# Fourier branch folded by symmetry, 20 modulation blocks moved, one bank wait shortened

## The reference, cut to what matters

```python
hl = modulate(rms_norm(xl, g_mix_norm[l]), sh1, sc1)
pl = hl @ wl                              # q, k, v and a Fourier part fl of 4 groups x 128
mix_l = concatenate([diff_attention(ql, k_all, v_all, lam, g_subln[l], lambda_init),
                     fourier_mix(fl, w_fourier[l])], axis=-1)
xl = xl + gt1 * (mix_l @ w_out[l])
...
def fourier_mix(f, w_fourier):
    fg = f.reshape(b, n, 4, 128).astype(float32)
    fr = fft2(fg, axes=(1, 3), norm='ortho').real       # over 512 tokens and 128 channels
    return einsum('bngc,gcd->bngd', fr, w_fourier).reshape(b, n, 512)
...
mod = silu(c) @ ada_w[i] + ada_b[i]       # second block: 6 x 1024 values, 48 blocks of 128
```

## Time and profile before

| | before |
|---|---|
| median of 3 runs | 2212.67 us |
| the profiled execution's own time | 2213.58 us |
| its span | 2211.9 us |
| mean granted PE clock | 0.992 |
| ACT busy | 702.6 us (32%) |
| DMA moved | 434.71 MB |
| first scores of the attention steps | 118 us from the start |

### The profile page before, as it was taken

How to read it: one execution, slowest core, us unless ns; L and a number is a source line. 1 busy time by engine, 2 the same in 40 slices (tenths; PEclk the granted TensorE clock), 3 DMA queues, 4 the chain that set the end, 5 groups by cost and what they waited for, 6 DMA issues and landing times.

```text
span 2211.9 us, 24806 instructions
## 1 busy us (share of the span) xinstructions
PE 2134.6 (97%) x9914; PEld 1428.7 (65%) x9914; DVE 1215.4 (55%) x1726; ACT 702.6 (32%) x1059; POOL 148.8 (7%) x157
## 2 busy tenths in 40 slices
PE   7999998997999989999999999999999999999997
PEld 3454444333333335678888888878777788888886
DVE  1776863344433336895474555566986646343434
ACT  4123422110000005323242231346884424232331
POOL 0011100002310004000000000000110000000000
PEclk9999999999999999999999999999999999999999
DMA  9756465999999993211345454423342222222221
GB/s 389 288 185 215 142 241 208 401 427 427 420 426 426 428 427 127 79 68 62 133 160 186 156 177 163 143 77 116 126 156 81 96 95 77 95 95 95 95 96 57
DMA packets 112808, 434.71 MB, mean 197 GB/s; under 512 B 7982, under 2 KB 13106, under 8 KB 98760
## 3 DMA queue, kind: packets, MB, share of 16 engines
q1 hardware_dynamic: 92872, 361.46, 42.6%
q0 software_dynamic: 19840, 71.93, 9.0%
HBM read 430.57 MB, written 6.36 MB: 198 GB/s over the span
## 4 chain that ended last, share of the span: by engine, by line
PE 60%; PEld 15%; DVE 7%; DMA 7%; issue 6%; ACT 2%; DVEq 2%; POOLq 0%; SPq 0%; PEldq 0%; POOL 0%; ACTq 0%
PE PS L1132 7%; PE PS L740 6%; PE PS L743 6%; PE PS L744 6%; PE PS L840 6%; PEld PS L740 5%; PEld PS L744 5%; PEld PS L743 4%; DMA work<-in_w_dn 4%; PE PS L1155 4%; PE PS L1399 3%; PE PS L1403 3%; PE PS L1402 3%; PE PS L1169 2%; PE PS L969 2%
## 5 line engine op out<-in xcount | busy, mean ns | idle before, releaser
L744 PE MATMUL PS<-work_f32r,work_f32r 128*128 128x512 f32 x1168 | 454.4, 389 | 0.0
L2155 DVE TENSOR_TENSOR ring_f32r<-ring,work_f32r 128x2048 fp32r<-128x2048 f32 x100 | 227.8, 2287 | 140.5 <-ACT work_f32r L1553 140.1
L740 PE MATMUL PS<-work_f32r,work_f32r 128*128 128x512 f32 x768 | 299.5, 390 | 2.1 <-DVE work_f32r L2902 1.1
L743 PE MATMUL PS<-work_f32r,ring_f32r 128*128 128x512 f32 x768 | 298.8, 389 | 0.0
L1553 ACT ACTIVATE work_f32r<-ring 128x2048 fp32r<-128x2048 f32 x100 | 190.2, 1910 | 304.0 <-DMA ring<-in_mlp_w 247.0
L744 PEld LDWEIGHTS PS<-work_f32r,work_f32r 128*128 128x128 f32 x1168 | 219.3, 188 | 45.6
L1132 PE MATMUL PS<-work 128*64 128x512 f32 x752 | 170.6, 597 | 2.2 <-ACT work L1761 2.2
L740 PEld LDWEIGHTS PS<-work_f32r,work_f32r 128*128 128x128 f32 x768 | 144.2, 188 | 33.3 <-DVE work_f32r L2902 1.5
L743 PEld LDWEIGHTS PS<-work_f32r,ring_f32r 128*128 128x128 f32 x768 | 144.2, 188 | 29.8 <-issue 0.2
L740 PE MATMUL PS<-h_f32r,work_f32r 128*128 128x512 f32 x400 | 155.9, 390 | 1.4 <-DVE work_f32r L2175 1.4
L743 PE MATMUL PS<-h_f32r,ring_f32r 128*128 128x512 f32 x400 | 155.6, 389 | 0.0
(11 more groups left out here) (423 smaller groups left out, 3357.8 us busy)
## 6 DMA issues: line engine op xcount, KB each, us to landing
work<-in_w_gu SPq DMA_DIRECT2D x47, 2048.0 KB, 21.9
ring<-in_mlp_w SPq DMA_DIRECT2D x64, 1024.0 KB, 5.2
work<-in_w_dn SPq DMA_DIRECT2D x24, 2048.0 KB, 24.6
ring<-in_w_gu SPq DMA_DIRECT2D x16, 2048.0 KB, 24.2
work<-in_ada_w_2T POOLq DMA_DIRECT2D x48, 512.0 KB, 3.6
work<-in_ada_w_2T POOLq DMA_DIRECT2D x16, 1536.0 KB, 6.8
ring<-in_m_w_in SPq DMA_DIRECT2D x20, 1024.0 KB, 5.2
work<-in_w_adaT POOLq DMA_DIRECT2D x8, 2048.0 KB, 10.4
```

The lines of the kernel that those rows point to most:

```text
L740: mm = nc.tensor.matmul(PS[:, bank + k, :], f32r(w_of), f32r(hi(c)), start=first and c == 0, stop=False)
L743: nc.tensor.matmul(PS[:, bank + k, :], f32r(wlo), f32r(hi(c)), start=False, stop=False)
L744: mm = nc.tensor.matmul(PS[:, bank + k, :], f32r(w_of), f32r(lo(c)), start=False, stop=last and c == 3)
L2155: tt(f32r(ring[:, s, at, :]), ring[:, s, at, :], f32r(tiles[s][:, at, :]), ALU.subtract).then_inc(w_split, 1)
```

## The change

The diff has three parts.

1. **The Fourier branch is folded.** Tokens t and 512 − t have the same cosine and opposite sines. DVE forms sum and difference of the two halves (`fold_tokens`, three instructions of up to 255 columns for each group); PE then has 5 matmuls of 128 columns for the channels and 5 of 255 or 257 columns for the tokens, all in banks 0 and 1; ACT copies 512 and 257 columns; DVE makes the 512 output frequencies from 257 cosine and 255 sine ones (`unfold_frequencies`, two instructions, one operand in PSUM, one side read backwards). Group g now has its channels and tokens in step 9 + g and `mix_out` at the start of step 10 + g. The value projections are spread as 2, 1, 1, 1, 1 over steps 0 to 4 and the projections of the Fourier part stand in steps 5 to 8. Part of out_part(0, 1) moves from step 15 to step 13.
2. **20 of the 48 modulation blocks leave the steps.** The steps keep 28 (`BLOCKS_AT`). The other 20 are 10 pairs, loaded by POOL as 1024 KB each into two new buffers, the first two when head 2's product is done, pair j when pair j − 2 has been used. DVE works pairs 2c and 2c + 1 ahead of the addition of output chunk c, for c = 0 to 4. The addition of their bias and the gain that needs them move to the gated stage of the second block.
3. **The wait of bank 7.** `head_values` waits for `ovar_ready` (the end of `head_var`, which reads the bank) in place of `head_done`.

```diff
-ADA_BLOCKS = NMOD * KC
-ADA_DONE = ADA_LATE + ADA_BLOCKS
+ADA_IN_STEPS = 28
+ADA_PAIRS = (NMOD * KC - ADA_IN_STEPS) // 2
+ADA_DONE = ADA_LATE + ADA_IN_STEPS + ADA_PAIRS
...
-        dft_c, dft_s, dft_ch = wk(13312, TC, T), wk(15360, TC, T), wk(17408, 256)
-        fab, fre = wk(17664, 2, 4, 256), wk(19712, T)
+        dft_c, dft_s, dft_ch = wk(13312, 3, 257), wk(14088, 2, 255), wk(17408, 256)
+        f_odd, f_half, fab, fre = wk(14600, GROUPS, 256), wk(16648, GROUPS, P), wk(15624, 2, 4, P), wk(19712, T)
...
+        ada_pair = [wk(17664, 2, D), wk(30720, 2, D)]
...
+        FIRST_MIX = 9
...
+        def mirrored(v):
+
+            n = v.ap[-1][1]
+            return bass.AP(v.tensor, v.offset + n - 1, [v.ap[0], (-1, n)])
...
-            sp.wait_ge(ada_used, 2 + ADA_DONE)
+            sp.wait_ge(ada_used, 2 + ADA_LATE + ADA_IN_STEPS)
...
-            for q in range(ADA_BLOCKS):
+            for q in range(ADA_IN_STEPS):
                 pool.wait_ge(ada_used, 2 + ADA_LATE + max(q - 1, 0))
                 pool.dma_start(ada_block[q % 2], A["ada_w_2T"][0, q * P:(q + 1) * P, :]).then_inc(ada_loaded[q % 2], 16)
-
-
-            pool.wait_ge(zero_row_stored, 16)
-            pool.wait_ge(rows_stored, 16)
+            pool.wait_ge(pv_mm, HEADS - 1)
+            for j in range(ADA_PAIRS):
+                pool.wait_ge(ada_used, 2 + ADA_LATE + ADA_IN_STEPS + max(j - 1, 0))
+                pool.dma_start(ada_pair[j % 2], A["ada_w_2T"][0, (ADA_IN_STEPS + 2 * j) * P:(ADA_IN_STEPS + 2 * j + 2) * P, :]
+                               .rearrange("(n p) k -> p n k", p=P)).then_inc(ada_loaded[j % 2], 16)
+
+
+            pool.wait_ge(rows_stored, 32)
...
             def mix_channels(g):
+                pe.wait_ge(folded, g + 1)
                 if g:
-                    pe.wait_ge(fourier_evac, 4 * (g - 1) + FR)
+                    pe.wait_ge(fourier_evac, 3 * (g - 1) + FO)
                 else:
                     pe.wait_ge(in_mix, 16 * 6)
                     pe.wait_ge(qkv_evac, 22)
-                for t in range(TC):
-                    if g and t == 2:
-                        pe.wait_ge(fourier_evac, 4 * (g - 1) + FO)
-                    mm = nc.tensor.matmul(PS[:, t // 2, (t % 2) * 256:(t % 2 + 1) * 256], fT[:, g, t * P:(t + 1) * P],
-                                          dft_ch, start=True, stop=True)
-                    if t % 2:
-                        mm.then_inc(fourier_mm, 1)
-
-            def mix_tokens(g, tiles):
-                pe.wait_ge(fourier_evac, 4 * g + AB)
-                for t in tiles:
-                    nc.tensor.matmul(PS[:, 0, :], fab[:, g % 2, t, 0:P], dft_c[:, t, :], start=(t == 0), stop=False)
-                    mm = nc.tensor.matmul(PS[:, 0, :], fab[:, g % 2, t, P:2 * P], dft_s[:, t, :], start=False,
-                                          stop=(t == TC - 1))
-                if t == TC - 1:
-                    mm.then_inc(fourier_mm, 1)
+                even, odd, cosines, sines = fT[:, g, :], f_odd[:, g, :], dft_ch[:, 0:P], dft_ch[:, P:2 * P]
+                for t in range(2):
+                    nc.tensor.matmul(PS[:, 0, t * P:(t + 1) * P], even[:, t * P:(t + 1) * P], cosines, start=True, stop=True)
+                nc.tensor.matmul(PS[:, 0, 3 * P:4 * P], odd[:, P:2 * P], sines, start=True, stop=True)
+                nc.tensor.matmul(PS[:, 0, 2 * P:3 * P], odd[:, 0:P], sines, start=True, stop=False)
+                nc.tensor.matmul(PS[:, 0, 2 * P:3 * P], f_half[:, g, :], cosines, start=False, stop=True).then_inc(fourier_mm, 1)
+
+            def mix_tokens(g):
+                pe.wait_ge(fourier_evac, 3 * g + AB)
+                if g:
+                    pe.wait_ge(folded, GROUPS + g)
+                for t in range(3):
+                    nc.tensor.matmul(PS[:, 1, 0:257], fab[:, g % 2, t, :], dft_c[:, t, :], start=(t == 0), stop=(t == 2))
+                for t in range(2):
+                    mm = nc.tensor.matmul(PS[:, 1, 257:512], fab[:, g % 2, 2 + t, :], dft_s[:, t, :], start=(t == 0), stop=(t == 1))
+                mm.then_inc(fourier_mm, 1)
 
             def mix_out(g):
-                pe.wait_ge(fourier_evac, 4 * g + FR)
-                nc.tensor.matmul(PS[:, 1, :], wfour[:, g, :], fre, start=True, stop=True).then_inc(fourier_mm, 1)
+                pe.wait_ge(folded, GROUPS + g + 1)
+                nc.tensor.matmul(PS[:, 0, :], wfour[:, g, :], fre, start=True, stop=True).then_inc(fourier_mm, 1)
...
-                        pe.wait_ge(head_done, hd)
+                        pe.wait_ge(ovar_ready, hd)
...
-                if n in (9, 11, 12, 14):
-                    mix_out({9: 0, 11: 1, 12: 2, 14: 3}[n])
+                if FIRST_MIX < n <= FIRST_MIX + GROUPS:
+                    mix_out(n - FIRST_MIX - 1)
                 if n:
                     turn_weights(n - 1, 0)
...
+                elif n < 5:
+                    values(n + 1)
+                    if n == 4:
                         tile_done()
-                elif n in (8, 9, 11, 12):
-                    mix_channels({8: 0, 9: 1, 11: 2, 12: 3}[n])
-                elif n in (10, 13):
-                    mix_tokens({10: 1, 13: 3}[n], range(2, 4))
+                        tile_wait("in", 1, 1)
+                elif n < FIRST_MIX:
+                    to_mix(n - 5)
+                    if n == 8:
+                        tile_done()
+                elif n < FIRST_MIX + GROUPS:
+                    mix_channels(n - FIRST_MIX)
+                elif n == 13:
+                    tile_wait("out", 0, 0)
+                    pe.wait_ge(fourier_evac, 3 * 2 + FO)
+                    out_part(0, 1, OUT_ORDER[0:3])
                 elif n == 14:
-                    tile_wait("out", 0, 0)
                     pe.wait_ge(head_done, 2)
+                    pe.wait_ge(fourier_evac, 3 * 3 + FO)
                     out_part(0, 0, OUT_ORDER[0:5])
                 elif n == 15:
-                    pe.wait_ge(fourier_evac, 4 * GROUPS)
-                    out_part(0, 1, OUT_ORDER[0:6])
+                    out_part(0, 1, OUT_ORDER[3:6])
...
+                if FIRST_MIX <= n < FIRST_MIX + GROUPS:
+                    mix_tokens(n - FIRST_MIX)
...
+                act.wait_ge(fourier_mm, 3 * g + AB)
+                copy(fab[:, g % 2, :, :], PS[:, 0, :].rearrange("p (t n) -> p t n", n=P)).then_inc(fourier_evac, 1)
...
+                copy(fre[:, 0:257], PS[:, 1, 0:257]).then_inc(fourier_evac, 1)
...
+                if FIRST_MIX < n <= FIRST_MIX + GROUPS:
+                    mixed_out(n - FIRST_MIX - 1)
                     weights_turned(n - 1, 0)
+                if FIRST_MIX <= n < FIRST_MIX + GROUPS:
+                    mixed_channels(n - FIRST_MIX)
                 exps(n)
+                elif n < FIRST_MIX:
+                    projected(13 + n)
                     head_square(hd - 1)
                     weights_turned(n - 1, 1)
                     head_root(hd - 2)
+                if FIRST_MIX <= n < FIRST_MIX + GROUPS:
+                    mixed_tokens(n - FIRST_MIX)
...
+            def mod_pair(j):
+
+                dve.wait_ge(ada_loaded[j % 2], 16 * ((ADA_LATE + ADA_IN_STEPS) // 2 + j // 2 + 1))
+                for n in range(2):
+                    w, q = ada_pair[j % 2][:, n, :], ADA_IN_STEPS + 2 * j + n
+                    done = stt(w, w, 1.0, cond2[:], ALU.mult, ALU.mult, accum_out=mod2[:, 0, q:q + 1])
+                done.then_inc(ada_used, 1)
...
+            def fold_tokens(g):
+                dve.wait_ge(qkv_evac, 18 + g + 1)
+                early, late = fT[:, g, 1:T // 2], mirrored(fT[:, g, T // 2 + 1:T])
+                tt(f_odd[:, g, 1:T // 2], early, late, ALU.subtract)
+                nc.vector.tensor_copy(f_half[:, g, 0:1], fT[:, g, T // 2:T // 2 + 1])
+                tt(early, early, late, ALU.add).then_inc(folded, 1)
+
+            def unfold_frequencies(g):
+                dve.wait_ge(fourier_evac, 3 * g + UV)
+                early, late, odd = fre[:, 1:T // 2], mirrored(fre[:, T // 2 + 1:T]), PS[:, 1, 257:512]
+                tt(late, early, odd, ALU.subtract)
+                tt(early, early, odd, ALU.add).then_inc(folded, 1)
+
+            BLOCKS_AT = (2, 2, 2, 2, 2, 2, 2, 2, 0, 2, 3, 2, 0, 2, 2, 1)
             for n in range(HEADS * TC):
                 hd, qc = n // TC, n % TC
                 maxima(n)
                 if n == 0:
                     modulation((5, ADA_TILES // 2), -MOD_EARLY // 4, cond1, col("b_ada", 0, 48), mod1)
+                    nc.vector.memset(f_odd[:, :, 0:1], 0.0)
+                    nc.vector.memset(f_half, 0.0)
+                if FIRST_MIX - 3 <= n < FIRST_MIX + 1:
+                    fold_tokens(n - FIRST_MIX + 3)
                 if hd >= 2 and qc == 0:
                     head_var(hd - 2)
                 if hd and qc == 3:
                     head_out(hd - 1)
+                first, count = sum(BLOCKS_AT[:n]), BLOCKS_AT[n]
+                ahead = min(2, count) if n else 0
```

(61 more changed lines are left out.)

37 lines of the change are left out of this document (1 added, 36 removed).

## The result

The changed kernel takes 2234.45 us (median of four runs, 2232.16 to 2235.19) against 2213.02 us of the kernel before on the same chip: a ratio of 1.0095, interval 1.0077 to 1.0112. It is slower by 21.4 us; 2228 us (2212 to 2236) was forecast. The profiled execution took 2232.16 us, 18.6 more than the profiled one of before, with a span of 2230.4 us. Traces are compared with that one.

What follows compares the result with a forecast made beforehand. PE bounds the attention steps and output projection, DMA the expert stage. Steps -13.4, late chunk 3 +26.7, PE's clock +1.7 sum to +15.0 us on the median 2212.67: 2228 us, range 2212 to 2236.

Steps and rivals of the forecast that it cites:

- The steps: Attention steps: the last turning comes 13.4 us earlier, 25.7 us of PE time less 12.3 us of waits.
- The walk through the engines' orders: Attention steps: PE, DVE and ACT orders followed with known durations; 12.3 us of waits, with 2.4 in step 9.
- Rival 3: Attention steps: they give all of PE's time, 25.7 us; 2215 us, half-way 2221; chance 0.11.
- Rival 4: Attention steps: the fold does not speed them (slow backward reads, PE's clock falls), -5 instead of -13.4; 2236 us; chance 0.07.
- The lateness of chunk 3: Output projection: chunk 3 waits for pair 7, whose loads are slowed beside the expert tiles; PE is 26.7 us late.
- The packet rule: Output projection: POOL's and SP's queues share DMA one to one by packets, 130 beside 140, about 22 per us.
- The clock: Output projection: after the wait for chunk 3 PE runs at 0.52 of its clock and loses 1.7 us.
- DVE's own work, "6 us late" without loads: Output projection: with every load there, DVE's work alone has chunk 3 squared at 342.7 us, 6 us late.
- rival 2: Output projection: pairs come as fast as small blocks; -7.4 us in sum with no loads; about 2207 us; chance 0.10.
- Rival 1: Output projection: the queue does not slow the pairs; -13.4 + 12.7 + 1.7 = +1.0, 2214 us; chance 0.12.
- Parts at zero: Bank wait on the kernel before, gated-stage bias and gain (at most 0.5 us), and other small edits: 0 us.
- a router chunk 3 that waits under 12 us: Output projection: a sign that the forecast is wrong, PE's wait at the fourth router chunk being under 12 us.

Runs made afterwards that it cites:

- the root experiment: Changed kernel with ScalarE taking head 0's square root in step 8 before copying the last Fourier projection: 2229.53 us, ratio 1.0067.

## Why the prediction was right, and where its size was off

- **The steps: -13.4 forecast, -12.0 measured.** The walk through the engines' orders held. The last turning, forecast near 282 us, came at 282.20, but 1.5 us of that are the execution's earlier start. PE's waits in the steps add up to 13.5 us (forecast 12.3). The two largest are where it put them, 2.4 us at the end of step 9 (forecast 2.4) and 2.1 in step 10 (2.9), and the root experiment shows their cause in head 0's root. Rival 3, all of PE's 25.7 us, fails: even with the root first the steps give 16.6. Rival 4's slow backward reads fail too: a fold took 0.7 us between starts and an unfold 0.7, and an addition of 255 elements takes 0.41 to 0.42 us with one side backwards and 0.41 with none.
- **The blocks' worth in the steps** was not priced by itself. The fold alone gave 3.1 us, less than rival 4's 5 us. The walk had the freed DVE in it, so its sum was near, but the text says nowhere that most of it hangs on the moved blocks: it takes the steps' gain as the fold's.
- **The lateness of chunk 3: 26.7 forecast, 30.3 measured.** This is the term that was mis-sized. On the clock of the kernel before, PE's router work on chunk 3 starts 30.3 us later, at 353.41 + 13.54 = 366.95 us in place of 336.65. The packet rule held (139 to 134, and 120 to 114 with pairs of 8 KB rows), and the tiles' share of the loss is shown by holding them back: 15.9 us. What was off is the landing of pair 3. From my own issue times moved by the last turning, pair 2 should have landed at 324.7 us and pair 3 at 330.4; they landed by 326.5 and 333.8. From there on nothing was added: pair 7 was done 3.4 us later than forecast, as pair 3 had landed 3.4 later. Why pair 3 was late stays open. The tiles, whose end the forecast put at 328.3 us on this clock, had their last 10 packets after 330. That pair 4, issued at 329.20 us, took packets from pair 3, and that a landing ends behind its last packet, would explain the rest, but no run here takes these apart. The Trainium skill ("DMA: Bandwidth & Descriptors", Queues, rings and completion order) says that each DMA engine goes round its queues a whole packet at a time; the traces agree, with their numbers just given.
- **The clock: 1.7 forecast, 2.0 measured.** Three waits of 16.05, 5.90 and 5.95 us kept it at 0.50, but the slow work between them cost nothing, since PE waited for DVE there anyway. What counts is behind the last one: 0.9 us more for the router work on chunk 3 and 1.1 for the turning behind it, then the clock was full again. 30.3 + 2.0 are the 32.3 us of the projection, where 28.4 were forecast.
- **DVE's own work, "6 us late" without loads**, was also too small: the experiment without loads has 8.3. The router bias's wait of 1.73 us inside the chain, which the sum left out, is most of the difference. With 3.0 us for the clock that makes 11.3, and 12.0 - 11.3 leaves no gain: 2214.25 us with no loads at all. The 7.4 us that rival 2 sums for that case, and its 2207 us, are therefore wrong whatever the loads do.
- **Rival 1, an undisturbed queue, 2214 us.** Its condition was not met: pair 3 took 22.2 us. With the tiles held back, its 12.7 + 1.7 us in the projection can be compared with the 16.4 measured. That kernel takes 2223 us and not 2214 mainly because another 6.3 lie behind the routing; the prediction says nothing of what else uses SP's queue.
- **Parts at zero.** The bank alone 1.0001; the rest behind the routing is 1850.5 us against 1850.7, so the gated stage hides its three instructions, as forecast.
- **The signs.** "Some 25 us" between out_part(1, 1) and the fourth router chunk are 27.9 in three waits. The sign of being wrong, "a router chunk 3 that waits under 12 us", was badly put: that row alone waits 5.95 us, since most of the lateness had been waited for at chunk 1. In the chances, rival 1 and half of rival 3 make 0.175 and not 0.16.
- **The whole.** +18.6 us between the profiled executions for +15.0: 3.9 from the projection, 1.4 from the steps (no more than executions differ), less 1.5 of earlier start. The medians stand 21.4 apart; the last 2.8 us are runs' spread (the profiled execution was the shortest of the four), and nothing here divides them further. The direction and the place are the forecast's; the time is near the upper end of the range.

## What to carry to other kernels

Free time of an engine is a place for work only if the engines that follow it in order don't want its next result: put the work ahead of an instruction that is itself waiting, and check each place for what is loading then. Two engines that take turns must both be relieved: the fold and the moved blocks gave 3 us each and 12 together. A load moved into a quiet engine's time can stand beside a stream with larger packets, which then has most of the bytes. Holding that stream back isn't free either: it can end up ahead of something else on its own queue, here a store that the next stage waits for.

## What the runs showed of the hardware

- Two DMA queues share the engines by packets: 134 of 4.1 KB beside 139 of 14.7 KB, and 114 of 7 KB beside 120 of 15 KB. A load of 1 MB took 17 to 22 us beside the stream and 5.2 to 7.3 (median 5.3) without it; in rows of 8 KB it took 11.9 and 17.0 beside the stream.
- A store of 2 MB landed in 9.0 us, and in 27.8 behind eight loads of 2 MB issued on its queue in the 22 us before.
- An addition or subtraction of 255 elements took 0.41 to 0.42 us with one operand read backwards, the same with the result written backwards and one operand in PSUM, and 0.41 with all forward and one operand in PSUM; an addition of 512 elements forward, with a multiplication in it, takes 0.75 us.
- PE's clock stood at 0.50 (1.2 GHz) from 330 to 350 us, where PE worked 2 of every 10 us, and at 0.56 from 330 to 340 us without the loads, where it had been busy 4.7 us of the 10 before and was busy 7.3.
